# w_o as three products of highs and lows with its panels' lows made on GpSimd, and the delta rule's inverse turned on TensorE at levels 1 to 5

## What is computed (reference, cut)

```python
def gated_delta_rule(q, k, v, log_a, beta):
    ...
    m_low = jnp.where(strict, einsum('nbhid,nbhjd->nbhij', kb, kc) * decay, 0.0)
    lhs = m_low + jnp.eye(CHUNK)
    sol = lax.linalg.triangular_solve(lhs, rhs, left_side=True, lower=True, unit_diagonal=True)
    ...
def hybrid_mixer(...):
    o_dn  = rms_norm(o_dn, dn_norm_g)   * silu(dn_z)
    o_gla = rms_norm(o_gla, gla_norm_g) * silu(gl_g)
    return concatenate([o_dn, o_gla], -1) @ w_o          # 1024 x 1024 times 1024 x 1024
def first_block(...):
    y = hybrid_mixer(h, ...)
    x = layer_norm(ALPHA * x + (1.0 + gt_a) * y, ln1_g, ln1_b)
    h = x * (1.0 + sc_f) + sh_f
    y = conv_ffn(h, ...)
```

## Time and profile before

| | |
|---|---|
| median of 3 runs | 3106.85 us (3104.19 to 3108.26) |
| the profiled execution | 3101.53 us, span 3100.3 us |
| TensorE busy | 2968.1 us, 96% of the span |
| VectorE, ScalarE, GpSimd busy | 1532.9, 968.4, 735.6 us |
| the delta rule | from about 430 to 768 us |
| w_o | from about 795 to 916 us |

### The profile page before, as it was taken

One profiled execution on the slowest core, in us unless ns is written; L12 is line 12 of the kernel. 1 busy time (PEld: TensorE's weight loads), 2 busy tenths in 40 slices (PEclk: granted clock), 3 DMA queues, 4 the chain that ended last, 5 costly groups with the idle time before them and its releaser, 6 DMA issues.

```text
span 3100.3 us, 33010 instructions
## 1 busy us (share of the span) xinstructions
PE 2968.1 (96%) x13260; PEld 2188.3 (71%) x13260; DVE 1532.9 (49%) x2443; ACT 968.4 (31%) x1524; POOL 735.6 (24%) x469
## 2 busy tenths in 40 slices
PE   6999999999989999999998999999999999999998
PEld 2444467676447888888886678787755888888886
DVE  7335543332285545545448574676534333333335
ACT  1226632223112222222223761365544122222112
POOL 3101112221035444444441113111000222222221
PEclk9999999999999999999999999999999999999999
DMA  7210012221341211111113112202311111111111
GB/s 256 72 34 24 24 34 68 62 62 37 137 156 46 62 54 48 48 48 48 48 48 109 61 48 84 76 3 75 97 41 34 55 48 48 48 48 48 48 49 60
DMA packets 199751, 193.60 MB, mean 62 GB/s; under 512 B 16151, under 2 KB 147631, under 8 KB 199599
## 3 DMA queue, kind: packets, MB, share of 16 engines
q1 hardware_dynamic: 197968, 187.09, 19.3%
q10 hardware_dynamic: 1631, 4.40, 0.4%
HBM read 175.43 MB, written 13.89 MB: 61 GB/s over the span
## 4 chain that ended last, share of the span: by engine, by line
PE 81%; DVE 9%; ACT 6%; issue 2%; DMA 1%; POOL 1%; SPq 0%; ACTq 0%; DVEq 0%; POOLq 0%
PE bank L1206 58%; PE bank L1233 6%; PE bank L1537 2%; PE bank L1298 1%; PE bank L1339 1%; PE bank L1353 1%; PE bank L1362 1%; PE bank L1521 1%; DVE ffn_conv L2116 1%; PE bank L1491 1%; PE bank L1513 1%; PE bank L1175 1%; PE bank L1510 1%; DVE ffn_conv L2112 1%; PE bank L1199 1%
## 5 line engine op out<-in xcount | busy, mean ns | idle before, releaser
L1206 PE MATMUL bank<-ft_hi,panel_lo 128*128 128x512 f32 x1312 | 468.7, 392 | 3.0 <-DVE panel_lo L1627 3.0
L2812 POOL TENSOR_TENSOR panel_lo<-panel,panelm_hi 128x1024 fp32r<-128x1024 f32 x64 | 153.2, 2394 | 765.8 <-ACT panelm_hi L2414 765.8
L1206 PEld LDWEIGHTS bank<-ft_hi,panel_lo 128*128 128x128 f32 x1312 | 247.8, 189 | 55.5 <-DVE panel_lo L1627 3.3
L1206 PE MATMUL bank<-ft_hi,panel_hi 128*128 128x512 f32 x704 | 275.4, 391 | 4.3 <-POOL panel_lo L2812 4.3
L1233 PE MATMUL bank<-ft,panel 128*128 128x512 f32 x576 | 268.3, 603 | 7.4 <-ACT mod_part L2529 4.8
L1206 PE MATMUL bank<-ft_lo,panel_hi 128*128 128x512 f32 x704 | 275.2, 391 | 0.0
L2112 DVE TENSOR_SCALAR ffn_conv<-ffn_in,ffn_taps 128x512 f32<-128x512 f32 x88 | 114.0, 1295 | 287.9 <-ACT ffn_in L2669 287.9
L2378 DVE TENSOR_TENSOR resid<-resid,bank 128x512 f32<-128x512 f32 x256 | 174.7, 687 | 151.5 <-PE bank L1206 150.7
L2812 POOL TENSOR_TENSOR panel_lo<-panel,panel_hi 128x1024 fp32r<-128x1024 f32 x66 | 157.9, 2401 | 227.7 <-ACT panel_hi L2414 227.7
L1206 PE MATMUL bank<-ftm_hi,panelm_hi 128*128 128x512 f32 x512 | 200.2, 391 | 2.4 <-DVE ftm_lo L1776 2.4
L1206 PE MATMUL bank<-ftm_lo,panelm_hi 128*128 128x512 f32 x512 | 200.0, 391 | 0.0
(11 more groups left out here) (447 smaller groups left out, 5710.9 us busy)
## 6 DMA issues: line engine op xcount, KB each, us to landing
panel<-in_w_in SPq DMA_DIRECT2D x52, 512.0 KB, 3.7
panel<-in_w_ada SPq DMA_DIRECT2D x48, 512.0 KB, 3.9
panel<-in_ffn_w_up SPq DMA_DIRECT2D x44, 512.0 KB, 3.7
panel<-in_w_mlp_in SPq DMA_DIRECT2D x32, 512.0 KB, 3.9
panel<-in_w_mlp_out SPq DMA_DIRECT2D x32, 512.0 KB, 3.6
panel<-in_w_o SPq DMA_DIRECT2D x24, 512.0 KB, 3.6
panel<-in_w_out SPq DMA_DIRECT2D x24, 512.0 KB, 3.6
panel<-in_ffn_w_down SPq DMA_DIRECT2D x22, 512.0 KB, 3.6
```

The source lines that it names most:

```text
L1206: m = te.matmul(ps, a, b, start=(start and j == 0), stop=(stop and j == len(pairs) - 1))
L2812: pool.tensor_tensor(lo, k.view(p), hi.bitcast(F32), ALU.subtract).then_inc(*g.new("halved_lo", p))
```

## The change

Two parts. In the delta rule the product xt of levels 1 to 5 goes; in its place the unit left of the next level transposes `inv` on TensorE, and VectorE copies the upper half blocks out of the bank into `inv_t`. GpSimd's clearing of `prod` goes. In w_o the 24 panels are split (high on ScalarE, low on GpSimd) and so are the gated activations (`gated_split`: high on ScalarE, low on VectorE, 16 of 128x512 each); every product becomes three in float32r. The panels of w_o now rotate through four slots, their highs through slots 4 and 5 and one further place; ScalarE splits at most one panel ahead, GpSimd two. Cut to the core:

```diff
@@ delta_banks @@
     if s.startswith("left"):
-        return [(s,)]
+        return [(s,)] if s == "left1" else [(s,), ("turned", int(s[4:]) - 1)]
     if s.startswith("right"):
-        return [(s, what) for what in ("xt", "x")[:1 if s == "right6" else 2]]
+        return [(s, "xt" if s == "right6" else "x")]
@@ schedule @@
         k.unit("project", "gg", c, 1, p, used=p, last=("gg", c, 1))
+        k.unit("gated_split", c, 0)
+        k.unit("gated_split", 4 + c, 0)
+    made = [k.panel("w_o", (0, h, 0), rows_of(d["w_o"][0], 0, 2 * P, h * BANK, BANK), True) for h in range(2)]
+    k.unit("ahead", used=made[0])
     for c in range(4):
         k.unit("z_gate", c, 1)
         k.unit("gg_gate", c, 1)
+        k.unit("gated_split", c, 1)
+        k.unit("gated_split", 4 + c, 1)
@@ memory, panel @@
+    k.wo_hi = place("wo_hi", [P, KD, T], F32R, at=at(12))
+    k.mixed_lo, k.g_lo = place("mixed_lo", [P, 4, T], F32R, at=at(8)), place("g_lo", [P, NT, BANK], F32R, at=at(20))
...
-        slot = self.in_ring(tuple(range(4 if stage in WIDE else SLOTS)))
+        slot = self.in_ring(tuple(range(4 if stage in WIDE or stage == "w_o" else SLOTS)))
...
+            elif stage == "w_o":
+                high = self.in_ring((4, 5, "False 0"))
@@ tensor_program: token_source, to_tokens, delta left and right @@
         if stage == "w_o":
-            return [k.mixed[:, kk, tile(n)] if kk < 4 else k.g_v[:, n, tile(kk - 4)]]
+            return [k.wo_hi[:, kk, tile(n)], k.mixed_lo[:, kk, tile(n)] if kk < 4 else k.g_lo[:, n, tile(kk - 4)]]
...
-                    pe.wait_ge(*(("z_gated", kk, hh) if kk < 4 else ("gated", kk - 4, hh)))
+                    pe.wait_ge("gated_lo", kk, hh)
...
             fill(m, "delta", n, s)
+            if lv > 1:
+                turned(("delta", n, "turned", lv - 1), lambda h: t.inv[:, h, :])
...
             if lv == 1:
                 pe.wait_ge("delta_dve", n, "inv_t")
             else:
-                pe.wait_ge(*pe.evicted("delta", n, f"right{lv - 1}", "xt"))
-            if lv < 6:
-                pe.wait_ge("delta_pool", n, "zero", lv)
-            ps = free("delta", n, s, "xt")
-            for h in range(H4):
-                if lv < 6:
-                    m = te.matmul(ps[:, h * GC:(h + 1) * GC], t.prod[:, h, :], blocks(t.inv_t, lv, 1)[:, h],
-                                  start=True, stop=True)
...
+                pe.wait_ge(*pe.evicted("delta", n, "turned", lv - 1))
@@ vector_program: gated_split, delta left @@
+    def gated_split(kk, h):
+        v.wait_ge("gated_hi", kk, h)
...
+        dve.tensor_tensor(lo, x, hi, ALU.subtract).then_inc(*v.new("gated_lo", kk, h))
...
+            v.wait_ge(*v.filled("delta", n, "turned", lv))
+            x = blocks(t.inv_t, lv, 1)
+            ps = heads(("delta", n, "turned", lv)).rearrange("p h (n two c) -> p h n two c", two=2, c=1 << lv)
+            evict(dve.tensor_copy(x, ps[:, :, :, 1, :]), "delta", n, "turned", lv)
@@ scalar_program: halve, gated_split, before @@
+        elif k.panel_list[p][0] == "w_o" and k.high_at[p] not in (4, 5):
+            a.wait_ge("z_gated", 1, 0)
+            a.wait_ge("z_gated", 0, 1)
...
+    def gated_split(kk, h):
+        a.wait_ge(*(("z_gated", kk, h) if kk < 4 else ("gated", kk - 4, h)))
...
+        act.activation(hi, x, ACT.Copy).then_inc(*a.new("gated_hi", kk, h))
...
-        while split_turn[0] < len(splits) and split_turn[0] <= k.split_index[used] + (3 if k.panel_list[used][0] in ("w_out", "cq") else SPLITS - 1) and \
+        while split_turn[0] < len(splits) and split_turn[0] <= k.split_index[used] + (3 if k.panel_list[used][0] in ("w_out", "cq") else 1 if k.panel_list[used][0] == "w_o" else SPLITS - 1) and \
@@ same_group; gpsimd_program: delta left @@
+    return k.panel_list[p][0] == k.panel_list[q][0] == "w_o" or \
...
-            if lv == 1:
-                g.wait_ge(*g.evicted("delta", n, "kq"))
-            else:
-                g.wait_ge(*g.filled("delta", n, f"right{lv - 1}", "x"))
-            if lv < 6:
-                pool.memset(blocks(t.prod, lv, 1), 0.0).then_inc(*g.new("delta_pool", n, "zero", lv))
```

More of the change, by code:

```diff
@@ L429, in schedule @@
         (2, 4): f2[0:1], (2, 5): f2[1:2], (2, 6): f2[2:4],
-        (2, 7): [lambda: norm_start(k, 1, (6, 7)), *a3, *rows((4, 5))]})
+        (2, 7): [lambda: norm_start(k, 1, (6, 7)), *a3, *rows((4, 5))]}, split=True, made=made)
     w_up, w_down = d["ffn_w_up"][0], d["ffn_w_down"][0]
@@ L1364, in delta @@
                 fill(m, "delta", n, s, "x")
+            else:
+                ps = free("delta", n, s, "xt")
+                for h in range(H4):
+                    m = te.matmul(ps[0:GC, h * GC:(h + 1) * GC], t.prod[:, h, 0:GC], t.inv_t[:, h, GC:P], start=True,
+                                  stop=True)
+                fill(m, "delta", n, s, "xt")
         elif s == "carry":
@@ L1856, in z_gate @@
         dve.tensor_tensor(o, o, k.z[:, c, half(h)], ALU.mult).then_inc(*v.new("z_gated", c, h))
+    def gated_split(kk, h):
+        v.wait_ge("gated_hi", kk, h)
+        hi = k.wo_hi[:, kk, half(h)].bitcast(F32)
+        if kk < 4:
+            x, lo = k.mixed[:, kk, half(h)], k.mixed_lo[:, kk, half(h)]
+        else:
+            x, lo = (t[:].rearrange("p n (c t) -> p c n t", c=4)[:, kk - 4, 4 * h:4 * h + 4, :] for t in (k.g_v, k.g_lo))
+            hi = hi.rearrange("p (n t) -> p n t", t=P)
+        dve.tensor_tensor(lo, x, hi, ALU.subtract).then_inc(*v.new("gated_lo", kk, h))
     def to_tokens(stage, h, k0, n_k, tiles, p):
@@ L1972, in delta @@
             evict(dve.tensor_tensor(t.inv[:], ID4, heads(("delta", n, "lt")), ALU.subtract), "delta", n, "lt")
+        elif s.startswith("left"):
+            lv = int(s[4:]) - 1
+            if lv == 0:
+                return
+            if lv == 1:
+                done("inv_t")
+            else:
+                v.wait_ge(*v.evicted("delta", n, "turned", lv - 1))
+            v.wait_ge(*v.filled("delta", n, "turned", lv))
+            x = blocks(t.inv_t, lv, 1)
+            ps = heads(("delta", n, "turned", lv)).rearrange("p h (n two c) -> p h n two c", two=2, c=1 << lv)
+            evict(dve.tensor_copy(x, ps[:, :, :, 1, :]), "delta", n, "turned", lv)
         elif s.startswith("right"):
             lv = int(s[5:])
-            def half_bank(what):
-                ps = v.bank("delta", n, s, what)[:, 0:H4 * GC]
-                return ps.rearrange("p (h n c) -> p h n c", h=H4, c=1 << lv)
             if lv < 6:
@@ L1982, in delta @@
                 x = blocks(t.inv, lv, 0)
-                evict(dve.tensor_tensor(x, x, half_bank("x"), ALU.subtract), "delta", n, s, "x")
-            if lv == 1:
-                done("inv_t")
-            else:
-                v.wait_ge(*v.evicted("delta", n, f"right{lv - 1}", "xt"))
-            v.wait_ge(*v.filled("delta", n, s, "xt"))
-            if lv < 6:
-                x = blocks(t.inv_t, lv, 1)
-                evict(dve.tensor_tensor(x, x, half_bank("xt"), ALU.subtract), "delta", n, s, "xt")
-            else:
+                ps = v.bank("delta", n, s, "x")[:, 0:H4 * GC].rearrange("p (h n c) -> p h n c", h=H4, c=1 << lv)
+                evict(dve.tensor_tensor(x, x, ps, ALU.subtract), "delta", n, s, "x")
+            else:
+                v.wait_ge(*v.evicted("delta", n, "turned", 5))
+                v.wait_ge(*v.filled("delta", n, s, "xt"))
                 x = t.inv_t[0:GC, :, GC:P]
@@ L2414, in halve @@
         act.activation(k.halves_of(p)[0], k.view(p), ACT.Copy).then_inc(*a.new("halved_hi", p))
+    def gated_split(kk, h):
+        a.wait_ge(*(("z_gated", kk, h) if kk < 4 else ("gated", kk - 4, h)))
+        hi, x = k.wo_hi[:, kk, half(h)], k.mixed[:, kk % 4, half(h)]
+        if kk > 3:
+            hi, x = hi.rearrange("p (n t) -> p n t", t=P), \
+                k.g_v[:].rearrange("p n (c t) -> p c n t", c=4)[:, kk - 4, 4 * h:4 * h + 4, :]
+        act.activation(hi, x, ACT.Copy).then_inc(*a.new("gated_hi", kk, h))
     def mix_split(c, h):
@@ L2776, in mlp_in @@
         act.activation(k.mlp_hid[c][0][:, half(h)], k.mlp_sq[h][:], ACT.Copy).then_inc(*a.new("mlp_hi", i, c, h))
-    a.run(dict(mix_split=mix_split, keep=keep, unit_length=unit_length, barrier=barrier, vectors=vectors, condition=condition, ada_out=ada_out, conv_silu=conv_silu,
+    a.run(dict(gated_split=gated_split, mix_split=mix_split, keep=keep, unit_length=unit_length, barrier=barrier, vectors=vectors, condition=condition, ada_out=ada_out, conv_silu=conv_silu,
                piece_out=piece_out, z_gate=z_gate, gg_gate=gg_gate, rab=rab, squares=squares,
```

10 lines of the change are left out of this document (2 added, 8 removed).

## The result

The changed kernel takes 3122.78 us (median of 6 runs, 3120.02 to 3124.61) against 3107.56 us for the kernel before (6 runs, 3104.19 to 3111.35): ratio 1.0048, 95% interval 1.0035 to 1.0061. It is 15.2 us slower. The forecast was +3.9 us. The profiled execution took 3124.3 us, with a span of 3123.1.

What follows compares the result with a forecast made beforehand. TensorE, 81% of the chain, was taken as the bound. Terms -17 (delta rule), +3 (start, group 0, norm), +17.4 (groups 1 and 2) and +0.5 gave +3.9 us on 3106.85: 3110.8, named 3110, range 3088 to 3128.

Steps and rivals of the forecast that it cites:

- likeliest case: Whole kernel: TensorE waits in w_o for GpSimd's lows; from -6 to +13 us, 3101 to 3120 us; chance 48%.
- rival (c): w_o: VectorE's queue, slowed beside GpSimd's lows, delays group 2's features; w_o costs 27 to 30 us, total 3125; chance 22%.
- Part 1: Delta rule: transposes instead of the product xt take 17.8 us from TensorE, of which 17 us are won.
- my end of 10 us: Delta rule: the low end of the gain, 10 us, if the copy gets stuck behind VectorE's bursts.
- Part 2: w_o's own products: 384 in float32r at 0.227 us, 87.2 us instead of 110.1, so -22.9 us.
- The start: Start of w_o: TensorE begins 6.1 us later, after splits, high and low; 1.4 us more before panel 2.
- The norm: Behind w_o's group 0: three VectorE additions slowed 1.4 us each beside lows; start, group 0 and norm together +3 us.
- Groups 1 and 2: w_o from the first features on: lows come late, TensorE waits 6.7 and 5.4 us for two panels; +17.4 us.
- The ring: w_o, group 1: feat_part, ft_hi, high, low and odd low wait in turn; 6.4 us against 3.8 of TensorE.
- The tail: Stage behind w_o: 17.7 us as today, with ada panels starting two units later; +0.5 us.

Runs made afterwards that it cites:

- turn_twice: delta_only with each of the 40 groups of four transposes issued twice into the same bank; 3108.73 us against 3106.93 for the kernel before, 1.0007.
- delta_only: The kernel before with the delta rule's half of the change alone, w_o untouched; 3097.31 us against 3108.08 for the kernel before, 0.9967.
- act_two: The changed kernel with ScalarE allowed two w_o panels ahead instead of one, from the second panel on; 3116.11 us, 1.0026 against the kernel before.
- adds_late: The changed kernel with GpSimd's additions to resid of tiles 0 to 3 moved behind the first FFN products; 3122.2 us, 1.0046 against the kernel before.
- lows_tiny: The changed kernel with w_o's lows made for 16 of 1024 columns only, products reading the high instead; 3094.87 us against 3109.12 for the kernel before, 0.9957.
- wo_only: The kernel before with w_o's half of the change alone, delta rule untouched; 3132.47 us against 3108.08 for the kernel before, 1.0078.
- delta_adds: delta_only with GpSimd's additions to resid of tiles 4 and 5 moved behind w_o; 3098.09 us against 3108.14 for the kernel before, 0.9969.

## Why the prediction was right and wrong

The range (3088 to 3128) held the time, and the likeliest case had the mechanism. The result lies above that case's own -6 to +13 and 12.8 us above the 3110 that I named, near rival (c), 3125. Of (c)'s mechanism part came true: VectorE had the norm of group 1 ready at t = 54.5, where my case had 47 and (c) 54 or later. But TensorE itself came to these transposes no earlier (918.3 us), and its one wait for the features of group 2 is 2.9 us, against 1.5 before.

**Part 1, the step that failed: -17, measured -10.8** (interval -14.0 to -6.5; -9.5 to -13.5 in the traces). The 17.8 us left TensorE's queue and the copy took 0.42 us where I had 0.41, but "time taken from TensorE there is mostly won" was mis-sized: I put it at 17 of 17.8, the runs show 10.8, and turn_twice prices added time at 0.7. I read the 19 us of gaps as what is left over; they are also what grows when the covering work goes. In delta_only TensorE is idle for 24.4 us of the stage against 20.3 before, and the low clock takes 6.8 us against 6.2. The mechanism of my end of 10 us (the copy stuck behind VectorE's bursts) is not what shows: waits for inv_t are 1.4 us in all.

**Part 2, the products.** A low clock apart, right: products at 0.227 us, group 0 in 48.0 us with 47.8 worked out, and its end 1.9 us earlier behind gg's end, with 1 worked out.

**The start: a wait of 6.1, measured 5.10;** 1.4 before panel 2, measured 1.37.

**The norm: start, group 0 and norm together +3, measured +6.2.** I counted three meetings of 1.4 us; there were four with 1.67 on average, 2.5 us more of the 3.2 missing, and TensorE waited for 10.2 us where I had 7. The 2.13 us of the earlier trace rows was one meeting that began late in the GpSimd instruction, and I took it for the mean. The Trainium skill (SBUF — State Buffer, section "SBUF: two separate sides") calls the shared ports an exclusive lock held for the whole instruction. The four ends 0.55 us behind the low's end agree. My estimate from it, up to 1.7 us for a meeting, was wrong as a bound: two of the four cost 1.98 and 2.18. As a mean it was the better of the two numbers.

**Groups 1 and 2: +17.4, measured +19.3.** The ring turned in 6.2 us (6.4 predicted). With t from the first feat_part, lows 12 to 16 end at t = 5.7, 11.9, 19.1, 28.7 and 39.2, where I had 5.8, 12.1, 18.4, 27.8 and 38.4. TensorE waited longest for panels 15 and 16, 4.14 and 5.97 us, against 6.7 and 5.4. GpSimd was busy for 75% from low 12 to the end of w_o, where I had over 85%: it was full only from 883 to 908 us. act_two shows that the ring, adds_late that the additions are causes, and lows_tiny gives the price of the lows in all. w_o as a whole was forecast at +20.9; wo_only has +24.4 with an interval of 20.5 to 28.0.

**The tail: +0.5, measured +0.2.**

So the sum missed by 11 us, 6 of them in the delta rule's term and 3.5 in w_o's. The rest is within the spread of the runs.

Of all versions run, the delta rule's half alone is the fastest that computes everything: 3097.31 us, 0.33% under the kernel before, with delta_adds level. Whether w_o's three products can pay with a schedule in which GpSimd's additions and lows both have room stays open. lows_tiny shows only that in this order of work taking the lows away is not enough: the additions, the start and the norm stay, and what a schedule without their waits would give was not measured.

## What to carry to other kernels

Before work is given to an idle engine, follow its queue through the stage with the durations of the trace and hold each result against the time at which its user wants it: GpSimd was 25% busy overall, and 20.0 of 20 us where it counted. Price time that is freed on a nearly full engine by adding the same amount again and measuring, since gaps grow when the work that covers them goes; and look at several executions, since the clock alone moved this stage by 4 us. A deadline that is relieved by moving work needs a look at the next deadline of the same queue.

## What the hardware showed that was not expected

Very small VectorE instructions are held too while GpSimd works. Newton steps of 128x2 in act_two, timeline of VectorE, with GpSimd's low beside the second:

```profile
899.92 1.75 DVE L1730 TENSOR_SCALAR newton<-moments 128x2 f32<-128x2 f32 x1
901.70 0.17 DVE L1731 TENSOR_SCALAR newton<-newton 128x2 int32<-128x2 int32 x1
...
902.50 2.35 DVE L1736 SCALAR_TENSOR_TENSOR rstd<-newton,rstd 128x2 f32<-128x2 f32 x1
...
906.06 5.72 DVE L1751 TENSOR_SCALAR xhat<-resid,moments,rstd 128x1024 f32<-128x1024 f32 x2
...
902.43 2.40 POOL L2845 TENSOR_TENSOR panel_lo<-panel,panel_lo 128x1024 fp32r<-128x1024 f32 x1 [0.79 <-ACT panel_lo L2436]
```

Two steps of 0.17 us take 1.75 and 2.35, each ending 0.02 to 0.04 us behind a low (899.25 to 901.63, 902.43 to 904.83), and two xhat 5.72 us instead of 1.53. A multiplication that reads a bank (L1890) keeps its 0.69 us beside a low, and so do the statistics (L1708) with 0.62 each. It holds the other way too, by which came first: the low at 879.57 takes 3.37 us instead of 2.39 behind a VectorE multiplication that ran until 880.74, and one addition to resid in group 0 (838.45) that began 0.14 us ahead of a low keeps its 0.69 us while the low takes 2.81. And the clock adds to the price of waits: behind each of w_o's four waits of 4 us or more the products are 0.43 instead of 0.227 us apart for 3 to 7 us.
